# The odd layer's attention placed between its own products, and the rotary tables beside the FFN

## The reference, cut to what matters

```python
def odd_mixer(x, positions, w_in, q_norm_g, w_q_b, kv_norm_g, w_kv_b, w_out):
    p = x @ w_in                       # 768 for q, 256 for kv, 32 rotary columns of k
    cq, ckv, k_pe = ...
    q = (rms_norm_2(cq, q_norm_g) @ w_q_b).reshape(B, S, 16, 64 + 32)
    kv = (rms_norm_2(ckv, kv_norm_g) @ w_kv_b).reshape(B, S, 16, 64 + 64)
    q_nope, q_pe = q[..., :64], q[..., 64:]
    k_nope, v = kv[..., :64], kv[..., 64:]
    ang = positions[..., None] * inv_freq
    q_pe = apply_rope(q_pe, cos(ang), sin(ang))     # pairs (x1, x2) are turned by the angle
    k_pe = apply_rope(k_pe, cos(ang), sin(ang))     # one k_pe for all 16 heads
    o = block_causal_mla_attention(q_nope, q_pe, k_nope, k_pe, v)
    return o.reshape(B, S, 1024) @ w_out
```

## Time and profile before

| | us |
|---|---|
| median of 3 runs | 2609.71 |
| the profiled execution | 2609.72 |
| its span | 2607.9 |
| TensorE busy in it | 2412.5 (93%) |
| VectorE, ScalarE, GpSimd busy | 1055.0, 896.7, 238.2 |
| mean granted clock of TensorE | 0.951 of full speed |

### The profile page before, as it was taken

The page is one execution under the profiler, slowest core; times in us unless marked ns, Lnnn a source line. Parts: engine busy times, 40 slices in busy tenths (PEclk is TensorE's granted clock), DMA queues, the critical chain, the costliest instruction groups (busy, mean ns, idle before and its releaser), DMA issues. The chain is left out here.

```text
span 2607.9 us, 34685 instructions
## 1 busy us (share of the span) xinstructions
PE 2412.5 (93%) x14168; PEld 2010.9 (77%) x14168; DVE 1055.0 (40%) x1516; ACT 896.7 (34%) x1559; POOL 238.2 (9%) x300
## 2 busy tenths in 40 slices
PE   5999999999999968969997999999996889999997
PEld 5787778888888856748896988888874668888886
DVE  2232226444433432536646533333534336333333
ACT  4343334333223321333322422222442554322223
POOL 3000000000000020004320400000400002200001
PEclk8999999999999975989999999999997889999998
DMA  4312113233333300400001233333230003233330
GB/s 115 97 50 56 41 44 105 70 109 97 94 97 89 89 9 1 113 18 1 0 1 49 69 102 105 95 92 96 74 73 29 1 0 105 75 107 99 94 95 33
DMA packets 351832, 175.49 MB, mean 67 GB/s; under 512 B 43638, under 2 KB 347940, under 8 KB 351692
## 3 DMA queue, kind: packets, MB, share of 16 engines
q1 hardware_dynamic: 351260, 172.41, 23.6%
q0 software_dynamic: 432, 1.09, 0.2%
HBM read 171.35 MB, written 2.11 MB: 67 GB/s over the span
## 5 line engine op out<-in xcount | busy, mean ns | idle before, releaser
L484 PE MATMUL acc<-act_hi,w_hi 128*128 128x512 f32 (+1 forms) x1808 | 659.5, 365 | 31.8 <-DVE act_lo L793 17.8
L485 PE MATMUL acc<-act_lo,w_hi 128*128 128x512 f32 (+1 forms) x1808 | 654.0, 362 | 0.0
L486 PE MATMUL acc<-act_hi,w_lo 128*128 128x512 f32 (+1 forms) x1808 | 653.9, 362 | 0.0
L467 DVE TENSOR_TENSOR w_lo<-w,w_hi 128x1024 fp32r<-128x1024 f32 (+1 forms) x326 | 398.7, 1227 | 467.9 <-ACT w_hi L460 467.7
L460 ACT ACTIVATE w_hi<-w 128x1024 fp32r<-128x1024 f32 (+1 forms) x326 | 335.6, 1034 | 368.6 <-PE acc L486 314.2
L484 PEld LDWEIGHTS acc<-act_hi,w_hi 128*128 128x128 f32 x1808 | 345.5, 191 | 90.3 <-DVE w_lo L467 23.3
L485 PEld LDWEIGHTS acc<-act_lo,w_hi 128*128 128x128 f32 x1808 | 345.2, 191 | 51.2
L486 PEld LDWEIGHTS acc<-act_hi,w_lo 128*128 128x128 f32 x1808 | 345.0, 191 | 51.2
L484 PE MATMUL acc<-hid_hi,w_hi 128*128 128x512 f32 (+1 forms) x768 | 280.8, 366 | 0.0
L486 PE MATMUL acc<-hid_hi,w_lo 128*128 128x512 f32 (+1 forms) x768 | 279.7, 364 | 0.0
L485 PE MATMUL acc<-hid_lo,w_hi 128*128 128x512 f32 (+1 forms) x768 | 279.1, 363 | 0.0
(11 more groups left out here) (426 smaller groups left out, 3043.7 us busy)
## 6 DMA issues: line engine op xcount, KB each, us to landing
...
```

Of the source, the lines that this page charges most:

```text
L467: e.tensor_tensor(w_lo[:, 0:part.n], w.raw[part.g % w.LOADS][:, 0:part.n], w_hi[:, 0:part.n].bitcast(F32), ALU.subtract).then_inc(w.lo.sem, 1)
L484: e.matmul(s.acc, *first, start=(k == 0), stop=False)
L485: e.matmul(s.acc, *second, start=False, stop=False)
L486: last = e.matmul(s.acc, *third, start=False, stop=(k == kt - 1))
```

## The change

`attention_stage` and `rope_stage` are gone. The odd layer now uses the hook `Attention`, and a new hook `Rope`, in the same Gemm as its products.

- **Order of the products.** The values come first (`v0`, `v1`: token jobs, which give them with tokens on the partitions, so no transposes), then for each quad of four heads its `kn` (2 tiles), `qr` (1 tile, the rotary part of q) and `qn` (2 tiles). `kn` and `qn` are kept by `KeepHeads` directly in the operands of the scores.
- **The units** of quad 0 lie beside the products of quad 1, those of quad 1 beside quad 2, those of quad 2 beside quad 3, spread over the five subs by their lengths; the 16 units of quad 3 follow the last product. The first unit of each quad stands ahead of the first matmul of the next `kn`.
- **The tables** of cosine and sine are built by VectorE in 13 steps, one per sub, from the tenth sub of the FFN's first product on, and by two ScalarE sines after them.
- **The rotation.** Pairs are swapped by two DMAs from GpSimd's queue instead of a matmul, turned by three VectorE instructions, and placed into the score operands by further GpSimd DMAs: 8 for `k_pe` and 4 for each quad's `qr`. VectorE waits for the swap's DMAs at the sub named by `behind`; TensorE waits for the placing DMAs ahead of a quad's first unit.

The diff, cut to its core:

```diff
-def attention_stage(core, iterations, q, k, v, out, scale, mask=None, near=None, rope=None, placed=None):
...
-        self.core, self.start, self.step = core, start, step
+    TURN, VALUES, OUT = 2, 3, 5
+
+    def __init__(self, core, bank, places, queries, keys, values, out, bias, ready, before=None):
+        self.core, self.UNITS = core, len(places)
+        self.PAIRS = self.UNITS // 8
+        last, step = places[-1], places[-1] - places[-2]
+        self.places = list(places) + [last + step * (n + 1) for n in range(self.OUT + 1)]
         self.queries, self.keys, self.values, self.out, self.bias, self.ready = queries, keys, values, out, bias, ready
...
+
+    def gpsimd_first(self, e):
+        e.dma_start(self.pos[:, :], self.positions[0].partition_broadcast(P)).then_inc(self.loaded.sem, 16)
+        e.dma_start(self.rate[:, :], self.freq).then_inc(self.loaded.sem, 16)
...
+    def gpsimd(self, e):
+        for x, swapped, there, _, places, _, (swaps, turned, placed) in self.tiles:
+            e.wait_ge(*there)
+            for two in range(2):
+                e.dma_start(swapped[two:P:2, :], x[1 - two:P:2, :]).then_inc(swaps.sem, 16)
+            e.wait_ge(*turned.at(3))
+            for rows, dst in places:
+                e.dma_start(dst, x[rows, :]).then_inc(placed.sem, 16)
+
+    def vector_after(self, e, n):
+        step = n - self.first
+        if 0 <= step <= self.STEPS:
+            self.table_step(e, step)
+        for x, swapped, there, behind, _, scale, (swaps, turned, _) in self.tiles:
+            if n == behind:
+                e.wait_ge(*there)
+                e.wait_ge(*self.table.at(2))
+                e.wait_ge(*swaps.at(32))
+                e.scalar_tensor_tensor(out=swapped, in0=swapped, scalar=scale, in1=self.sine[:, :], op0=ALU.mult,
+                                       op1=ALU.mult).then_inc(turned.sem, 1)
+                e.scalar_tensor_tensor(out=x, in0=x, scalar=scale, in1=self.cosine[:, :], op0=ALU.mult, op1=ALU.mult)\
+                 .then_inc(turned.sem, 1)
+                e.wait_ge(*turned.at(2))
+                e.tensor_tensor(x, x, swapped, ALU.add).then_inc(turned.sem, 1)
...
+    def table_step(self, e, step):
+        ts, stt = e.tensor_scalar, e.scalar_tensor_tensor
+        angle, turns, shifted, over = (x[:, :] for x in (self.angle, self.turns, self.shifted, self.over))
+        if step == 0:
+            e.wait_ge(*self.loaded.at(32))
+            ins = e.tensor_copy(angle, self.pos[:, :])
+        else:
+            e.wait_ge(*self.made.at(step))
...
+    def scalar_after(self, e, n):
+        if n == self.first + self.STEPS + 1:
+            e.wait_ge(*self.made.at(self.STEPS + 1))
+            e.activation(self.cosine[:, :], self.shifted[:, :], ACT.Sin).then_inc(self.table.sem, 1)
+            e.activation(self.sine[:, :], self.angle[:, :], ACT.Sin, scale=self.sign[:, 0:1]).then_inc(self.table.sem, 1)
...
-def rope_stage(core, A, qr, k_pe):
...
-            add("kn", KD, 2, heads(kv_b, 2, 0, HD, 4), group=4)
-            add("v", KD, 2, heads(kv_b, 2, HD, HD, 4), group=4)
-            add("qn", KD, 6, heads(q_b, 6, 0, HD))
-            add("qr", 4, 6, heads(q_b, 6, HD, ROPE))
+            for n in range(2):
+                jobs[f"v{n}"] = TokenJob(w, f"v{n}", 2, lambda k, n=n: [
+                    (i, 1, 0, T, kv_b[:, i, 8 * n:8 * n + 8, HD:2 * HD]) for i in range(2)])
+            for quad in range(4):
+                add(f"kn{quad}", 2, 2, heads(kv_b, 2, 2 * quad, 0, HD, 2), group=2)
+                add(f"qr{quad}", 1, 6, heads(q_b, 6, quad, HD, ROPE))
+                add(f"qn{quad}", 2, 6, heads(q_b, 6, 2 * quad, 0, HD))
 
```

and of the stage itself:

```diff
+    for name, epilogue in (("kv", Keep(tile_of(o, 6))), ("k_pe", Keep(lambda u: k_pe)), ("q", Keep(tile_of(o)))):
+        J[name].bind(act, normed, epilogue)
+    for n in range(2):
+        J[f"v{n}"].bind(operand_of(kv_hi, kv_lo), kv_normed, Keep(lambda u, n=n: v[:, u, n * T:(n + 1) * T]))
+    scale = (HD + ROPE) ** -0.5
+    for quad in range(4):
+        J[f"kn{quad}"].bind(operand_of(kv_hi, kv_lo), always, KeepHeads(lambda h, quad=quad: ks[:, quad % 2, h, :]))
+        J[f"qr{quad}"].bind(act, q_normed, Keep(lambda u, quad=quad: qr[:, quad % 2, :]))
+        J[f"qn{quad}"].bind(act, always, KeepHeads(lambda h, quad=quad: qs[:, quad % 2, h, :], scale=scale))
+    names = ffn.names + ["kv", "k_pe", "q", "v0", "v1"] + [f"{s}{quad}" for quad in range(4) for s in ("kn", "qr", "qn")]
+    g = Gemm(core, ctx, [J[name] for name in names], norms=("up00", "kv"), first_parts=1, few_banks=J["kn1"], bank=bank)
...
+    rope = Rope(core, ctx, A, values_at, g.start_of(J["up00"]) + 9)
+    last_q = g.last_sub(J["q"], 5)
+    rope.add(k_pe[:, :], swapped[:, 1, :], g.act_of(last_q), v0 + 3,
+             [(slice(HD, HD + ROPE), ks[HD:HD + ROPE, slot, h, :]) for slot in range(2) for h in range(4)], scale)
+    for quad in range(4):
+        sub = g.last_sub(J[f"qr{quad}"], 0)
+        rope.add(qr[:, quad % 2, :], swapped[:, quad % 2, :], g.act_of(sub), sub.n + 1,
+                 [(slice(32 * h, 32 * h + 32), qs[HD:HD + ROPE, quad % 2, h, :]) for h in range(4)])
+
+    def ready(e, n):
+        if n % 16 == 0:
+            e.wait_ge(*g.act_of(g.last_sub(J[f"qn{n // 16}"], 1)))
+            if n == 0:
+                rope.wait(e, 0)
+            rope.wait(e, n // 16 + 1)
...
+    places = []
+    for quad in range(1, 4):
+        first = g.start_of(J[f"kn{quad}"])
+        span = [(first + n, t) for n, t in enumerate((1.4, 1.4, 4.1, 4.1, 4.1))]
+        places += places_over(span, 16)
+    places += [len(g.subs) + n / 16 for n in range(16)]
+    mla = Attention(core, bank[2:8], places, of_quad(qs), of_quad(ks),
+                    lambda kt, head: v[:, kt, HD * head:HD * head + HD], tile_of(o), causal, ready)
+    g.run(ffn.lead, ffn.first_norm, ffn.second_norm, kv_norm, q_norm, rope, mla)
...
 def second_block(core, A):
     with ExitStack() as c:
         o = even_layer(core, A, c)
-        with ExitStack() as r:
-            kn_v = core.sb(r, "mla_kn_v", [P, 2 * KD, T], side="right")
-            hid_at = core.nc.sbuf_top
-            qn = core.sb(r, "mla_qn", [P, KD, T], side="right")
-            qn_at = core.nc.sbuf_top
-            qr = core.sb(r, "mla_qr", [P, 4, T], side="right")
-            k_pe = core.sb(r, "mla_k_pe", [P, 1, T], side="right")
-            with ExitStack() as p:
-                activations(core, p)
-                even_out_to_mla(core, p, o, kn_v, hid_at, qn, qn_at, qr, k_pe)
-            rope_stage(core, A, qr, k_pe[:, 0, :])
-            attention_stage(core, 2, two_tiles(qn), two_tiles(kn_v), two_tiles(kn_v, KD), one_tile(o), (HD + ROPE) ** -0.5,
-                            core.chunk_mask, rope=(one_tile(qr), k_pe[HD:HD + ROPE, 0, :]))
+        with ExitStack() as p:
+            even_out_to_mla(core, p, A, o)
         with ExitStack() as p:
             activations(core, p)
             odd_out(core, p, o)
```

446 lines of the change are left out of this document (114 added, 332 removed).

## The result

The changed kernel takes 2562.74 us (median of 4 runs, 2555.5 to 2564.4) where the kernel before takes 2609.5; the ratio is 0.982, with a 95% interval of 0.9808 to 0.9833. The forecast was 2560, from 2546 to 2585. The profiled execution has a span of 2562.7 us (2607.9 before), so 45.2 us have to be found in it.

The account below looks back on a forecast made before the run. After the products, TensorE's own work and the idle and slow time around it were taken to bound the kernel. Terms (a) to (g) sum to 125.9 us in place of 175.9, 50.0 less: 2609.7 to 2560 us, range 2546 to 2585.

Parts of the forecast that it names:

- (a): First quad's rotation through GpSimd: TensorE stalls 5.5 us before the first scores, plus 2.0 of clock; 7.5 us, from 4 to 24.
- (b): 48 attention units between the odd layer's products, at the first block's 1.52 us each: 73.0 us, upper bound 77.3.
- (d): Collisions: VectorE's splits and rotation delay maxima between units at 1.3 us per quad; 4 us in all, from 0 to 12.
- (c): Three quad boundaries: first scores wait for ScalarE to keep the last `qn` tile, about 1.8 us each, 5.4 in all.
- (e): The last 16 attention units, with nothing beside them, at 1.61 us each: 25.8 us.
- (f): The drain from the last score to the kept attention output: 7.7 us before, 6.8 forecast.
- (g): The next stage's start, ahead of `odd_out`'s first matmul: unchanged at 3.4 us.
- The FFN at nothing: Rotary table work beside the FFN's products costs 0, at most 7 us if the cover fails; products end as before.
- R1: First quad's rotation chain is long: stall 15 to 20 us, 2572 to 2580; chance 0.21, shared with milder boundary losses.
- R2: No collisions between units and products: (a) at 4, (c) at 1.3 each, (d) at 0, 2551 us; chance 0.15.
- R3: TensorE's stops at quad boundaries and rotations each bring 25 us at half clock, losing 12.5: 2645 us; chance 0.03.
- R4: Latency from scores to exponential, not TensorE, sets the unit's step at 3.23 us: 63 more, 2623 us; chance 0.02.

## Why the prediction was right, step by step

The sum was 125.9 us from the last product to `odd_out`. In the changed kernel the products of before would end at 1981.7 + 6.3 = 1988.0 and `odd_out` begins at 2112.3: 124.3. The terms, one by one:

- **(a) The first rotation**, 7.5 forecast: the wait is 6.8 and the clock behind it lost some 3 (0.50 for 5 us and a little more), 9.8. The chain was the one named, with the small issue price. Mis-sized were two things that ended within 0.44 us of each other. The swap's landing took 4.6 us where 2.1 had been taken, behind eight placings in flight. And I had VectorE turn as soon as the swap landed, while its queue held a low half of weights ahead; once k_pe was out of the way, that alone was worth 2.6 us (5.51 to 2.92).
- **(b) and (d), 48 units and collisions**, 77.0 forecast. 2077.1 - 1950.4 = 126.7 us, less 198 products at 0.2333 (46.2), three waits (4.6) and clock missing behind the first and second wait (3.0 and 1.7): 71.2, or 1.48 a unit, and in it 1.6 us of waiting for exponentials. The first block's step carries over. It had come out as 1.52 with products at 0.227, but that block's products run at the slow pace too, and with 0.2333 the same rows give 1.47. The 4 us for collisions were 1.6. That the step is TensorE's own work is borne out by the units in a row, which take no longer.
- **(c) Boundaries**, 5.4 forecast: 3 x 1.53 = 4.6, ended by ScalarE's last kept tile.
- **(e) The last 16 units**, 25.8 forecast: 23.3 us for the starts from 2077.13 to 2100.43, and 1.6 for the last, 24.9. **(f) and (g)**, 10.2 forecast: 2112.3 - 2102.0 = 10.3.

These are 120.8. The 1.7 us of clock at one boundary, which the sum had left out, and 1.4 for the slower pace of the 216 q products bring them to 123.9 of the 124.3.

**The FFN at nothing, at most 7 us.** The reason given (ScalarE and VectorE have room for the tables) held: leaving the tables out changes nothing. The step that failed is the sentence under it, that the products are "the same number of matmuls" and so end when they did. It took their 0.227 us as fixed, though in the trace of before the `kn` matmuls are 0.2333 us apart and those of q 0.2267, and I put both down as one. The price was 6.3 + 1.4 = 7.7 us, for which the forecast had no term; without it the changed kernel would stand near 2555. That the median came within 3 us of 2560 is in part luck: the odd layer had gained 1.6 us more than forecast, and the wide range took the rest.

**The rivals.** R1 (a stall of 15 to 20 us): the landings of the rotation's DMAs were 1.8 to 4.6 us, and it did not come. R2 (no collisions) was nearly right in (c) and (d), but not in (a). R3 (the clock): the stops did bring stretches at half clock, of 5 to 12 us and not 25, and not each time; by TensorE's busy time 5.2 us of clock were missing in the odd layer against 22.8 before, so what would have sunk the change is where a third of its gain came from. The kernel before has both kinds of stretch in its attention stage, units alone each time:

```profile
2046.00:2081.00 35.00, 33.24 (x241) 26.50 (x239) 13.02 (x27) 20.61 (x61) 0.00 (x0) 1.00 0.01 2
2081.00:2112.00 31.00, 22.67 (x96) 16.83 (x97) 9.12 (x18) 19.00 (x43) 0.00 (x0) 0.67 0.00 0
```

The first has only waits of 0.25 to 0.58 us in it and stays at 1.00; the second begins with the loop's second staging, has waits of 0.9 to 3.9 us, and falls. The rule of the Trainium skill's page "TensorE: Matmul & The Clock Gate", section "A second HAM failure mode: psum-queue depth-cycling", by which many small pauses make the clock oscillate, is not borne out by these rows: the low clock came with the longer stops. R4 (latency): no. The rule of the Trainium skill's page "SBUF — State Buffer", section "SBUF: two separate sides", by which a DMA issued from GpSimd looks blocked while VectorE holds both ports, shows in no row here: an issue took 0.49 to 0.57 us, and while the late swap was in flight VectorE stood idle for 3.85 us.
